# LayerNorm statistics computed per token in five columns and spread back by products, with early buffers for one weight chunk

## The chip, the cores and the metric

The kernel runs on one core of one Trainium2 chip. The metric is the device time of one execution in microseconds (us), as the median of several runs; lower is better.

## What is computed

One inference step of a two-layer decoder for 512 prompt tokens and 8 sample tokens that share every weight. Each layer has three sub-layers (a SwiGLU feed-forward, a token mixer, a second feed-forward), so there are six, numbered n = 0 to 5: n = 0, 2, 3, 5 are feed-forwards, n = 1 is the attention and retention mixer ("EVEN"), n = 4 the short convolution mixer ("ODD"). Around each of them:

```
h = x * (1 + scale) + shift                       # adaLN modulation
x = layernorm(ALPHA * x + gate * sublayer(h)) * g + b
def layernorm(x): mu = mean(x); var = mean((x - mu)^2); (x - mu) * rsqrt(var + eps)
swiglu(h) = (silu(h @ w_a) * (h @ w_b)) @ w_out
```

D is 1024, the feed-forward width 2816. All is float32.

## The kernel before

**Layout.** x lies in SBUF with features on the partitions: 8 tiles of 128 features (KT = 8), each tile 520 tokens wide, split in two halves of 260 so that a half fits a PSUM bank. All products have tokens as the moving operand, 260 columns at a time.

**Products.** To keep float32 accuracy each operand is split in two float32r parts: hi (rounded, by ScalarE) and lo (the rest, by VectorE for activations and GpSimd for weights), and three products hi*hi, hi*lo, lo*hi are added in PSUM (`product`, L707). Weights come in chunks of 128 output columns: SyncE loads a chunk into raw[k], ScalarE cuts w_hi[k] (L1219 to L1224), GpSimd cuts w_lo[k] (L665 to L669), TensorE uses it; there are two buffers, k = 0 and 1, in turn. Each sub-layer has a first product (into the sub-layer) and a second one (back to D), whose output tiles are added to x by VectorE (`residual`, L1545). In the second product of a feed-forward an output tile takes two chunks, in that of a mixer one. In n = 0, 2 and 3 TensorE also works on pieces of the adaLN matrix between the chunks (L731, L740), and turns the last of their sums right after the norm's products (`turn_group`, L720).

**The norm's statistics.** While the second product runs, VectorE adds the tiles up in tile_sum (L1568). After half of the tiles an approximate mean, `shift`, is made from a product with a 128 x 128 matrix of 1/D (mean_w), which adds over the partitions and spreads the result to all of them. With it VectorE makes x - shift (`distance`, L1570 to L1583), ScalarE squares it (L1186), VectorE adds the squares up in sq_sum. After the last tile, `norm_sums` (L815) makes mean and mean square of all 520 tokens, on all 128 partitions, in two pairs of PSUM banks. `norm_act` (L1188) copies the mean to SBUF. `norm` (L1606) on VectorE subtracts and squares (mean - shift), takes it from the mean square, centres tile 0, and takes the reciprocal of the root that ScalarE made (L1193): each of these works on 128 x 520 elements. GpSimd meanwhile centres tiles 1 to 7 (`centre`, L431; tile 7 after the samples of tile 0).

**Into the next sub-layer.** Per tile: VectorE multiplies x by rdev (`normalise_tile`, L1536), ScalarE makes h for the prompt tokens (L1213), GpSimd makes it for the 8 samples with two small instructions (L451, L454), ScalarE rounds it to h_hi (L1217), VectorE makes h_lo (`low`, L1541). TensorE's `first_products` (L744) takes the tiles as they come and works on the first two chunks at once, the second one four tiles behind (LAG = 4).

**Order of the work.** Every engine runs its own list of instructions in the order in which the program gives them, held only by semaphores. GpSimd's list at a boundary: cut the next product's chunk 0, cut its chunk 1 (`body(0)`, L694), centre, samples. ScalarE's: cuts of the two next chunks at the last two chunks' turns, the squares, norm_act, h and h_hi per tile. SyncE's list for EVEN (`even_loads`, L479): chunks 0 to 3, then the page table, then, after the waits at L503 and L504, eight pages of the key cache, then chunks 4 and 5. The pages lie in SBUF over the region R_ADA.

## Time and profile before

| | us |
|---|---|
| median of 3 runs | 2562.47 |
| lowest, highest | 2559.23, 2563.54 |
| the profiled execution | 2561.66 |
| its span, first to last instruction | 2559.8 |

The profile gives for each engine its busy time, the granted clock of TensorE (1.00 is full speed, 0.50 half), and for each instruction its start and duration. A chain view follows the last instruction back through what released each step. A timeline view lists instructions in order of time and merges equal neighbours: "x4" is four of them, and the duration is that from the first one's start to the last one's end. A float32 product appears as two matmul instructions. Durations of neighbours on one engine may overlap by a few hundredths of a microsecond.

### The profile page before, as it was taken

What the parts mean: (1) busy time and instruction counts of PE and PEld (TensorE: products, weight loads), DVE (VectorE), ACT (ScalarE), POOL (GpSimd) and SP (SyncE); (2) the same over time, 40 slices, a digit from 0 to 9 for tenths busy, and PEclk for the clock granted to TensorE, in tenths of its full rate; (3) what the DMA queues carried; (4) which work ended last, traced back from release to release, by engine and by line L of the source; (5) the groups of instructions that cost most, each with busy time, mean ns of one, the idle gap of its engine ahead of it and who ended that gap; (6) DMA issues with size and microseconds to landing.
All of it is one profiled execution on the core that took longest, in us unless ns stands there. A gap on an engine that the chain in (4) does not pass through costs nothing.

```text
span 2559.8 us, 44523 instructions
## 1 busy us (share of the span) xinstructions
PE 2381.1 (93%) x18440; PEld 2153.4 (84%) x18440; DVE 839.5 (33%) x1020; ACT 731.1 (29%) x1055; POOL 929.7 (36%) x473
## 2 busy tenths in 40 slices
PE   7999999989988988899999799999979987999996
PEld 2899988769964338899999799998869986999995
DVE  1122211337434655322212522220253445222214
ACT  3222211242222332422212432221233224222213
POOL 1344433334330014444433444443243435444442
PEclk9999999979986989999999999999989998999998
DMA  7133376526642532233364133347622321333331
GB/s 280 58 91 93 93 238 211 155 72 205 180 118 55 155 94 75 66 91 90 93 213 147 41 95 93 92 141 235 211 72 75 96 78 50 91 93 93 99 91 45
DMA packets 448317, 298.41 MB, mean 117 GB/s; under 512 B 20102, under 2 KB 422118, under 8 KB 448086
## 3 DMA queue, kind: packets, MB, share of 16 engines
q1 hardware_dynamic: 448214, 296.92, 38.0%
q8 instruction: 78, 1.28, 0.2%
q14 instruction: 25, 0.20, 0.0%
HBM read 291.36 MB, written 5.53 MB: 116 GB/s over the span
## 4 chain that ended last, share of the span: by engine, by line
PE 57%; DVE 6%; issue 4%; POOL 3%; ACT 1%; DMA 0%; POOLq 0%; DVEq 0%; SPq 0%; ACTq 0%
PE ps L715 49%; PE ps L740 1%; POOL w_lo L668 1%; POOL x L438 1%; PE ps L1022 1%; DVE sq L1577 1%; PE ps L976 1%; PE ps L972 1%; DVE sq_sum L1582 1%; POOL samp_t L451 1%; DVE x L1539 1%; PE ps L1029 0%; PE ps L727 0%; PE ps L997 0%; DVE rdev L1618 0%
## 5 line engine op out<-in xcount | busy, mean ns | idle before, releaser
L668 POOL TENSOR_TENSOR w_lo<-raw,w_hi 128x1024 fp32r<-128x1024 f32 (+1 forms) x308 | 807.7, 2624 | 1355.5 <-ACT w_hi L1224 1355.5
L715 PE MATMUL ps<-h_hi,w_hi 128*128 128x260 f32 x3584 | 727.3, 284 | 25.0 <-POOL w_lo L668 14.1
L715 PE MATMUL ps<-h_hi,w_lo 128*128 128x260 f32 x3584 | 725.7, 284 | 0.0
L715 PE MATMUL ps<-h_lo,w_hi 128*128 128x260 f32 x3584 | 724.9, 284 | 0.0
L1224 ACT ACTIVATE w_hi<-raw 128x1024 fp32r<-128x1024 f32 (+1 forms) x308 | 346.6, 1126 | 1209.2 <-PE ps L715 1128.4
L715 PEld LDWEIGHTS ps<-h_hi,w_hi 128*128 128x128 f32 x3584 | 556.5, 190 | 30.2 <-POOL w_lo L668 13.4
L715 PEld LDWEIGHTS ps<-h_hi,w_lo 128*128 128x128 f32 x3584 | 556.2, 190 | 0.0
L715 PEld LDWEIGHTS ps<-h_lo,w_hi 128*128 128x128 f32 x3584 | 555.2, 190 | 0.0
L715 PE MATMUL ps<-hid_hi,w_hi 128*128 128x260 f32 x1408 | 296.3, 292 | 0.0
L715 PE MATMUL ps<-hid_hi,w_lo 128*128 128x260 f32 x1408 | 284.1, 283 | 0.0
L715 PE MATMUL ps<-hid_lo,w_hi 128*128 128x260 f32 x1408 | 283.3, 283 | 0.0
L1905 DVE TENSOR_TENSOR gated<-silu_a,ps 128x520 f32<-128x520 f32 x88 | 61.3, 697 | 662.1 <-PE ps L715 646.7
L715 PEld LDWEIGHTS ps<-hid_hi,w_hi 128*128 128x128 f32 x1408 | 216.3, 189 | 47.4 <-issue 42.4
L1908 DVE TENSOR_TENSOR hid_lo<-gated,hid_hi 128x520 f32 (+1 forms) x88 | 204.3, 2322 | 81.9 <-ACT hid_hi L1466 81.9
L715 PEld LDWEIGHTS ps<-hid_lo,w_hi 128*128 128x128 f32 x1408 | 217.5, 189 | 0.0
L715 PEld LDWEIGHTS ps<-hid_hi,w_lo 128*128 128x128 f32 x1408 | 217.4, 189 | 0.0
L1552 DVE SCALAR_TENSOR_TENSOR x<-ps,mod,x 128x512 f32<-128x512 f32 x48 | 36.0, 751 | 538.5 <-PE ps L715 538.5
L756 PE MATMUL ps<-h_hi,w_hi 128*128 128x260 f32 x192 | 48.4, 338 | 61.2 <-DVE h_lo L1543 61.0
L756 PEld LDWEIGHTS ps<-h_hi,w_hi 128*128 128x128 f32 x192 | 33.9, 218 | 74.2 <-issue 58.9
L1577 DVE TENSOR_TENSOR sq<-x,shift 128x520 f32<-128x520 f32 x48 | 81.4, 1706 | 1.4
L740 PE MATMUL ps<-ada_w,c_act 128*32 128x256 f32 x960 | 76.1, 391 | 2.7 <-DMA ada_w<-w_ada 2.7
L684 POOL TENSOR_TENSOR proj<-proj 128x520 f32<-128x520 f32 x4 | 5.1, 1288 | 187.3 <-ACT hn_sq L1340 187.3
(284 smaller groups left out, 1888.0 us busy)
## 6 DMA issues: line engine op xcount, KB each, us to landing
raw<-w_ffn_in SPq DMA_DIRECT2D x176, 512.0 KB, 3.6
ada_w<-w_ada SPq DMA_DIRECT2D x120, 512.0 KB, 6.5
raw<-w_ffn_out SPq DMA_DIRECT2D x64, 704.0 KB, 4.5
pages<-cache_k SPq DMA_DIRECT2D x64, 256.0 KB, 2.9
pages<-cache_v SPq DMA_DIRECT2D x64, 256.0 KB, 2.9
raw<-w_in_even SPq DMA_DIRECT2D x28, 512.0 KB, 4.3
raw<-w_in_odd SPq DMA_DIRECT2D x24, 512.0 KB, 3.6
ada_first<-w_ada SPq DMA_DIRECT2D x5, 2048.0 KB, 14.4
```

What stands on the lines that cost most here:

```text
L438: eng.tensor_tensor(x[:, t], x[:, t], mean[:, :, :], ALU.subtract).then_inc(centred[part], 1)
L451: pool.tensor_tensor(two(samp_t[:, t]), x[:, t, :, HP:HT], two(mod[:, m, KT + t, 1:9]), ALU.mult).then_inc(samp_mod, 1)
L668: pool.tensor_tensor(w_lo[:, k, 0:kt, :], raw[:, k, 0:kt, :], w_hi[:, k, 0:kt, :].bitcast(F32), ALU.subtract).then_inc(chunk_cut, 1)
L715: mm = pe.matmul(ps[:, 2 * q + half, 0:HT], w[:, k, t, :], v[:, kt0 + t, half, :], start=start and t == 0 and step == 0, stop=stop and t = ...
L740: mm = pe.matmul(ps[32 * t:32 * t + 32, 7, 0:ADA_W], c_act[:, at, :], ada_w[:, q % NADA, t, :], start=at < KT // 2, stop=at >= KT // 2)
L756: mm = pe.matmul(ps[:, 2 * q + half, 0:HT], w[:, k, t, :], v[:, t, half, :], start=t == 0 and step == 0, stop=t == KT - 1 and step == 2)
L972: pe.matmul(ps[:, u % 2, 0:(j + 1) * 128], proj[r, QF + m, j * 128:(j + 1) * 128], proj[r, KF + m, 0:(j + 1) * 128], start=True, stop=True ...
L1224: act.activation(w_hi[:, k, 0:kt, :], raw[:, k, 0:kt, :], ACT.Identity).then_inc(hi_cut, 1)
L1552: dve.scalar_tensor_tensor(xt[:, :, 0:HP], ps[:, 2 * q:2 * q + 2, 0:HP], g[:, 0:1], xt[:, :, 0:HP], ALU.mult, ALU.add).then_inc(drained, 1)
L1577: dve.tensor_tensor(sq[:, t % 2], x[:, t], shift[:, :, :], ALU.subtract).then_inc(shifted, 1)
L1905: dve.tensor_tensor(gated[:, j], silu_a[:, j], pair(2 * j + 1), ALU.mult).then_inc(gate_done, 1)
L1908: dve.tensor_tensor(hid_lo[:, m].rearrange("p a h c -> p (a h) c"), gated[:, j], hid_hi[:, m].rearrange("p a h c -> p (a h) c").bitcast(F3 ...
```

## The change

The norm's sums are now made with tokens on the partitions: the data (128 features x 128 tokens) is the stationary operand and one column of mean_w the moving one, so that each product gives one column, and five of them cover the 520 tokens. The fifth block overlaps the fourth. The sum of the tiles is replaced by tile_dev = tile_sum - 8 * shift, made by VectorE before the last residual, whose sums with those of x tile 7 give mean - shift. Square, difference, root and reciprocal run on 128 x 5 elements. The reciprocal is spread back to all partitions, tokens along the free axis, by six products of its columns (broadcast) with parts of the identity, into a PSUM pair that `normalise_tile` then reads. The mean itself is still made by products with mean_w and copied to SBUF for the centring; its part of tile_sum no longer waits for the last tile. The add of square 6 moves ahead of the last residual. In n = 0 and 3 the last turn_group moves ahead of the spread. Chunk 1 of each next first product is loaded into early_raw and cut into early_hi and early_lo, in the region R_ADA, while the second product still runs: SyncE issues it before the last two chunks, ScalarE cuts it at the third chunk from the end, GpSimd right after the last chunk of the second product. ScalarE runs a root on a small tile at the last-but-one chunk. In EVEN, SyncE waits for both first chunks to be used before it loads pages.

```diff
+        early_raw = put("early_raw", [128, KT, 128], F32, R_ADA)
+        early_hi = put("early_hi", [128, KT, 128], F32R, R_ADA + 4096)
+        early_lo = put("early_lo", [128, KT, 128], F32R, R_ADA + 8192)
+        tile_dev = put("tile_dev", [128, 2, HT], F32, R_ADA + 3 * 4096 + 1024)
...
+        tok = new("tok", [128, 4, TB])
+        delta_sq, dev, root, rdev = (tok[:, u] for u in range(4))
...
+        def token_block(v, b):
+            at = min(128 * b, NTOK - 128)
+            return v.rearrange("p h c -> p (h c)")[:, at:at + 128]
...
+            def early_chunk(n):
+                if n + 1 < last:
+                    sp.dma_start(early_raw[:, :, :], early_view(n + 1)).then_inc(early_full, 16)
...
                 sp.wait_ge(ada_turned, groups_before(EVEN))
+                sp.wait_ge(chunk_used, c0 + 2)
                 for k in range(2):
                     granule(cache_k, 0, k)
...
+            def early_cut(n):
+                if n + 1 < last:
+                    pool.wait_ge(early_hi_cut, n + 1)
+                    pool.tensor_tensor(early_lo[:, :, :], early_raw[:, :, :], early_hi[:, :, :].bitcast(F32), ALU.subtract)
...
+                        second_body(KT // 2 - 1)
+                        early_cut(n)
                     else:
-                        body(0)
                         if n:
-                            centre(pool, n - 1, 1)
+                            cut(chunks_before(n), 0, KT, 2)
+                            centre(pool, n - 1)
...
             def norm_sums(n):
+                def per_token(bank, v, start):
+                    for b in range(TB):
+                        mm = pe.matmul(ps[:, bank, b:b + 1], token_block(v, b), mean_w[:, 0:1], start=start and b == 0,
+                                       stop=not start and b == TB - 1)
+                    return mm
                 pe.wait_ge(shift_ready, n + 1)
-                pe.wait_ge(samp_added, KT * (n + 1))
+                pe.wait_ge(summed, (KT - 1) * (n + 1))
                 for half in range(2):
                     pe.matmul(ps[:, 4 + half, 0:HT], mean_w, tile_sum[:, half, :], start=True, stop=False)
+                pe.wait_ge(delta_steps, 3 * n + 1)
+                per_token(0, tile_dev[:, :, :], True)
+                pe.wait_ge(samp_added, KT * (n + 1))
+                per_token(0, x[:, KT - 1], False).then_inc(mean_done, 1)
+                for half in range(2):
                     mm = pe.matmul(ps[:, 4 + half, 0:HT], mean_w, x[:, KT - 1, half, :], start=False, stop=True)
                 mm.then_inc(mean_done, 1)
                 pe.wait_ge(sq_added, (KT - 2) * (n + 1))
+                per_token(1, sq_sum[:, :, :], True)
+                pe.wait_ge(squared, KT * (n + 1))
+                per_token(1, sq[:, (KT - 1) % 2], False).then_inc(var_done, 1)
+                if ADAS[n]:
+                    turn_group(n, GROUPS * len(ADAS[n]) - 1)
+                pe.wait_ge(mean_ready, n + 1)
+                pe.wait_ge(centred[0], CENTRE * (n + 1))
+                pe.wait_ge(rdev_done, n + 1)
                 for half in range(2):
-                    pe.matmul(ps[:, half, 0:HT], mean_w, sq_sum[:, half, :], start=True, stop=False)
-                pe.wait_ge(squared, KT * (n + 1))
-                for half in range(2):
-                    mm = pe.matmul(ps[:, half, 0:HT], mean_w, sq[:, (KT - 1) % 2, half, :], start=False, stop=True)
+                    bank = 2 * spread_pair(n) + half
+                    for b, at, cols, out0 in (((0, 0, 128, 0), (1, 0, 128, 128), (2, 0, 4, 256)),
+                                              ((2, 4, 124, 0), (3, 0, 128, 124), (4, 120, 8, 252)))[half]:
+                        mm = pe.matmul(ps[:, bank, out0:out0 + cols], rdev[:, b:b + 1].to_broadcast([128, 128]),
+                                       ident[:, at:at + cols], start=True, stop=True)
...
-                        if not beyond or next_kt:
-                            cut(c0 + s + 2, u % 2, next_kt if beyond else kt)
+                        if not beyond:
+                            cut(n, c0 + s + 2, u % 2, kt)
+                        elif u % 2 == 0:
+                            act.activation(root, eps_ln[:, :].to_broadcast([128, TB]), ACT.Sqrt)
+                            if next_kt:
+                                cut(n, c0 + s + 2, 0, next_kt, 2)
+                        if s + 3 == KT * per_tile:
+                            early_cut(n)
...
-                dve.tensor_tensor(x[:, t], x[:, t], rdev[:, :, :], ALU.mult).then_inc(normed, 1)
+                dve.tensor_tensor(x[:, t], x[:, t], pair(spread_pair(n)), ALU.mult).then_inc(normed, 1)
...
+                    if t == KT - 1:
+                        dve.wait_ge(summed, (KT - 1) * (n + 1))
+                        dve.scalar_tensor_tensor(tile_dev[:, :, :], shift[:, :, :], -float(KT), tile_sum[:, :, :], ALU.mult, ALU.add
+                                                 ).then_inc(delta_steps, 1)
                     product_done(t // 2, t % 2)
...
                 dve.wait_ge(mean_ready, n + 1)
-                dve.tensor_tensor(shift[:, :, :], mean[:, :, :], shift[:, :, :], ALU.subtract).then_inc(delta_steps, 1)
-                dve.wait_ge(delta_steps, d0 + 1)
-                dve.tensor_tensor(shift[:, :, :], shift[:, :, :], shift[:, :, :], ALU.mult).then_inc(delta_steps, 1)
+                for t in range(CENTRE):
+                    dve.tensor_tensor(x[:, t], x[:, t], mean[:, :, :], ALU.subtract).then_inc(centred[0], 1)
+                dve.wait_ge(var_done, 2 * n + 1)
                 dve.wait_ge(delta_steps, d0 + 2)
-                dve.wait_ge(var_done, n + 1)
-                dve.tensor_tensor(dev, pair(0), shift[:, :, :], ALU.subtract).then_inc(delta_steps, 1)
-                centre(dve, n, 0)
+                dve.tensor_tensor(dev, ps[:, 1, 0:TB], delta_sq, ALU.subtract).then_inc(delta_steps, 1)
                 dve.wait_ge(dev_done, n + 1)
-                dve.reciprocal(rdev[:, :, :], dev).then_inc(rdev_done, 1)
-                dve.wait_ge(rdev_done, n + 1)
+                dve.reciprocal(rdev, root).then_inc(rdev_done, 1)
+                dve.wait_ge(var_done, 2 * n + 2)
```

## Rows read from the trace of the kernel before

**Rows 1.** The page: the chain that ended last, by engine.
```profile
PE 57%; DVE 6%; issue 4%; POOL 3%; ACT 1%; DMA 0%; POOLq 0%; DVEq 0%; SPq 0%; ACTq 0%
```

**Rows 2.** Timelines (start, us, engine), norm of n = 2: VectorE, ScalarE, GpSimd, ScalarE.
```profile
1439.34 0.17 DVE L1557 TENSOR_TENSOR x<-x,samp 128x8 f32<-128x8 f32 x1
...
1441.68 0.60 ACT L1190 ACTIVATE mean<-ps 128x520 f32<-128x520 f32 x1 [0.77 <-PE ps L822]
...
1442.41 9.32 POOL L438 TENSOR_TENSOR x<-x,mean 128x520 f32<-128x520 f32 x6
...
1455.80 0.64 ACT L1217 ACTIVATE h_hi<-h 128x520 fp32r<-128x520 f32 x1 [1.13 <-POOL h L454]
```

**Rows 3.** Narrow float32 products: TensorE's timeline, then the chain in order of time.
```profile
1432.42 0.51 PE L727 MATMUL ps<-res,ada_sums 128*128 128x9 f32 x4
...
748.12 4.41 PE ps L905 x20
```

**Rows 4.** TensorE's timeline, wide float32 products in the norm of n = 1.
```profile
1014.14 1.07 PE L822 MATMUL ps<-x,res 128*128 128x260 f32 x2
1015.01 1.07 PE L821 MATMUL ps<-tile_sum,res 128*128 128x260 f32 x2
```

**Rows 5.** Timelines of GpSimd and VectorE, single instructions, norm of n = 1.
```profile
1020.79 1.74 POOL L438 TENSOR_TENSOR x<-x,mean 128x520 f32<-128x520 f32 x1
1022.49 1.28 POOL L438 TENSOR_TENSOR x<-x,mean 128x520 f32<-128x520 f32 x1
...
1019.72 0.70 DVE L1615 TENSOR_TENSOR sq<-ps,shift 128x520 f32<-128x520 f32 x1
```

**Rows 6.** Timelines of GpSimd and ScalarE, tile 3 after the norm of n = 2.
```profile
1457.86 0.74 POOL L451 TENSOR_TENSOR samp_t<-x,mod 128x8 f32<-128x8 f32 x1 [1.65 <-DVE x L1539]
1458.68 0.54 POOL L454 TENSOR_TENSOR h<-samp_t,mod 128x8 f32<-128x8 f32 x1
...
1459.31 0.64 ACT L1217 ACTIVATE h_hi<-h 128x520 fp32r<-128x520 f32 x1 [0.68 <-POOL h L454]
```

**Rows 7.** TensorE's timeline, norm of n = 0; then ScalarE, h_hi of tile 1.
```profile
505.67 0.71 PE L821 MATMUL ps<-tile_sum,res 128*128 128x260 f32 x2
...
521.75 0.64 ACT L1217 ACTIVATE h_hi<-h 128x520 fp32r<-128x520 f32 x1 [1.13 <-POOL h L454]
```

**Rows 8.** VectorE's timeline, end of the second product of n = 1; then ScalarE, h_hi of tile 1.
```profile
1005.87 2.90 DVE L1577 TENSOR_TENSOR sq<-x,shift 128x520 f32<-128x520 f32 x1
...
1012.83 0.17 DVE L1557 TENSOR_TENSOR x<-x,samp 128x8 f32<-128x8 f32 x1
...
1030.16 0.64 ACT L1217 ACTIVATE h_hi<-h 128x520 fp32r<-128x520 f32 x1 [1.13 <-POOL h L454]
```

**Rows 9.** Timelines of SyncE, TensorE, ScalarE, TensorE, start of EVEN.
```profile
535.78 8.05 SPq L494 DMA_DIRECT2D pages<-cache_k  x8
...
538.57 0.48 PE L715 MATMUL ps<-h_hi,w_hi 128*128 128x260 f32 x2 [0.15 <-POOL w_lo L668]
...
549.25 1.06 ACT L1224 ACTIVATE w_hi<-raw 128x1024 fp32r<-128x1024 f32 x1 [3.34 <-DMA raw<-w_in_even]
...
552.19 0.17 ACT L1239 ACTIVATE proj<-ps 128x8 f32<-128x8 f32 x1
...
553.92 0.60 PE L852 MATMUL ps<-res,proj 128*8 128x128 f32 x4
```

**Rows 10.** Timelines of GpSimd, VectorE and ScalarE, the last norm (n = 5).
```profile
2527.74 11.06 POOL L438 TENSOR_TENSOR x<-x,mean 128x520 f32<-128x520 f32 x7 [14.88 <-ACT mean L1190]
...
2535.15 7.27 DVE L1539 TENSOR_TENSOR x<-x,rdev 128x520 f32<-128x520 f32 x8
...
2539.40 4.37 ACT L1203 ACTIVATE x<-x,params 128x520 f32<-128x520 f32 x6 [0.88 <-DVE x L1539]
```

**Rows 11.** Windows: stretch, us, busy PE, PEld, DVE, ACT, POOL (instructions), PEclk, DMA share, GB/s.
```profile
785.00:792.00 7.00, 7.00 (x129) 6.91 (x128) 2.75 (x7) 0.00 (x0) 0.00 (x0) 0.50 0.28 65
...
1018.60:1029.50 10.90, 0.00 (x0) 0.00 (x0) 9.73 (x8) 2.89 (x4) 10.77 (x10) 0.70 0.05 13
```

114 lines of the change are left out of this document (73 added, 41 removed).

## The prediction

> **What bounds the kernel now.** I read the page first: the chain that ended last runs through TensorE for 57% and through VectorE for 6% [rows 1], and most of that TensorE share is the dense products, which the change leaves as they are. So the question is what TensorE waits for between two sub-layers, six times. I then read the chain in order of time at each norm. In the mixers it leads through GpSimd's centring of six tiles, and ScalarE's rounding (h_hi) of tile 1 waits for GpSimd's sample instruction [rows 8]. The timelines of the engines show why: x tile 0 is centred by VectorE, but GpSimd makes the samples of tile 0 only after its six centrings, and every h_hi waits for its samples. In n = 2 the last sample add ends at T0 = 1439.51, the mean is copied at 1441.68, the six centrings run from 1442.41 to 1451.73, and the h_hi of tile 1 starts at 1455.80 [rows 2]. VectorE's own chain of 520-wide instructions ends at about the same time as the centrings, so both must get shorter for anything to be won. From there the tiles come at a pace that TensorE follows, and the time at which h_hi of tile 1 starts, plus the pace, sets the end. I price each norm by that start.
>
> **Prices.** A narrow float32 product (two records): 20 records of L905 take 4.41 at the low clock, 0.22 each; four records of L727 take 0.51 with the drain, which fits about 0.11 each at the full clock [rows 3]. So a block of five one-column products (10 records) costs 1.1 us at full clock and 2.2 at half. The width of the moving operand hardly enters; I take this from products of 8 and 9 columns, the nearest rows. A page of the Trainium skill speaks otherwise: "TensorE: Matmul & The Clock Gate", in the section "Part 1: The HAM clock gate", gives start-to-start times that fall with the width of the moving operand down to about 25 ns; by that a block would cost an estimated 0.25 us, and the sum would come out several us lower. The rows here, with a new stationary operand each time, do not bear it out, and I keep 0.11 and 0.22. Two 260-column records take 0.87 at the low clock (1014.14 to 1015.01), so four take 1.75, and 0.87 at full clock [rows 4]. A centring on GpSimd takes 1.74 when VectorE works beside it on two SBUF operands, and 1.28 beside the reciprocal, while VectorE's own instruction with one PSUM operand takes 0.70 in the midst of the centrings [rows 5]. So neither blocks the other there. After the change VectorE has only one SBUF-only wide instruction beside the centrings (tile 0): six of them take 1.8 + 5 x 1.24 (1.28 less the overlap) = 8.0 instead of 9.3.
>
> **n = 2.** TensorE ends its last product at about 1438.4 (T0 less the 1.1 us of the residual). Then: tile_sum, 0.9, to 1439.3; block of tile_dev, 1.1, to 1440.4; block of x tile 7, to 1441.5 (T0 is past); its four wide records, to 1442.3; copy of the mean, 0.7, to 1443.05, where before it ended at 1442.3. The first mean thus comes 0.8 later. Centrings to 1451.1. Samples of tile 0, 0.5; tile 7, 1.24; samples of tile 1 (the first behind h_lo of tile 0, 0.66, the second 0.28): h_hi of tile 1 at 1453.75 against 1455.80 [rows 2], a gain of 2.05. The statistics are hidden: 20 records for the squares to 1444.5, three small instructions, about 0.9 with their handovers, spread of 12 records 1.3 to 2.6, done by 1448.1 at the worst, 3 us before the centrings end. If that cover went, each further us would cost one.
>
> **The pace.** Two tiles take 3.51 (h_hi from 1455.80 to 1459.31). In that pair, tile 3 waits for two sample instructions of 0.74 and 0.54, the second held up by normalise_tile [rows 6]. With a PSUM operand the latter no longer holds the port, so 0.54 becomes 0.20: 0.34 less per pair, in two pairs; the last has no normalise_tile behind it. Gain 0.7 per norm. For n = 2 together -2.75.
>
> **n = 0 and 3.** Here TensorE still works on the adaLN pieces until 505.67 [rows 7]. From there 0.9, 1.1, 1.1, 0.9 and 0.7 give the mean at 510.35; centrings to 518.3; with 0.5, 1.24 and 0.94, h_hi of tile 1 at 521.0 against 521.75 [rows 7]. Gain 0.8 + 0.7 = 1.5 each, -3.0 for both. The moved turn_group (0.4) lies under the centrings.
>
> **n = 1 and 4, the mixers.** Their second product has one chunk per tile, and VectorE is behind TensorE: an SBUF-only subtract takes 2.90 because a weight cut of GpSimd has the port [rows 8]. The early cut comes just before and takes the port once more, 2.3 us of VectorE time, while the cut it replaces lay after T0. Add 6 before the last residual waits for its square (0.15) and takes 0.62, tile_dev 0.75. Behind VectorE's list stand the last residual and, for it, TensorE. T0 moves from 1013.0 [rows 8] by 3.8 to 1016.8. TensorE has by then been idle long enough that the clock is at its half level: in a stretch without any product its mean is 0.70, full at first and half for the rest [rows 11]. So: tile_dev to 1017.9, x tile 7 to 1020.05, wide records to 1021.8, mean 1022.5, centrings to 1030.5. The spread comes at 1021.8 + 4.3 + 0.9 + 2.6 = 1029.6, normalised tile 0 at 1030.3, again just covered. h_hi of tile 1: 1030.5 + 0.5 + 1.24 + 0.94 = 1033.2 against 1030.16 [rows 8], 3.0 later, less 0.7 of pace: +2.3 each, +4.6.
>
> **EVEN's pages.** The new wait moves the page loads from 535.78 to the end of the first two products, about 538.4 (TensorE starts the third at 538.57). Chunk 4 is queued behind them on SyncE; ScalarE cuts it at 549.25 having waited for its DMA, and only then copies chunks 2 and 3, to 552.36, which TensorE's L852 needs at 553.92 [rows 9]. 2.65 later is 1.1 late: +1.1. Were it hidden, 0; were more behind it, 2.65. The other queues: early chunks are as large as those they replace, are issued chunks ahead of their cuts, and cost nothing; the new root and its table load on ScalarE come a whole chunk before anyone waits for it.
>
> **The last norm.** By the steps of n = 2 the mean comes 0.7 later: seven centrings from 2528.4, in 9.25, to 2537.7 instead of to 2538.8. Before, normalising starts only at 2535.15 and takes 7.27 for eight tiles, and ScalarE's last affine ends at 2543.77 [rows 10]. Now the spread is there by 2532.2 to 2533.4, every tile follows its centring, the last affine ends at 2537.7 + 0.65 + 0.85 = 2539.2: -4.5.
>
> **Clock allowance.** The one-column products may not hold the clock up: in the stretch of 128 one-column products TensorE is busy 7.00 of 7.00 us and stays at 0.50 [rows 11]. If it falls in the middle of the blocks before the mean, 1 to 3 us per feed-forward norm; after the last dense product the full level outlasts part of an idle stretch [rows 11], and the blocks come first in it, so I add 1.0 in all.
>
> **Sum.** -2.75 - 3.0 + 4.6 + 1.1 - 4.5 + 1.0 = -3.5 against the profiled execution's 2561.66 (span 2559.8 and 1.9 around it). The median of the runs shown is 0.8 above that, so 2562.5 - 3.5 = 2559.0. About 0.2%, 5.1 us, is what a measurement of this kernel can tell from no change; this lies within it.
>
> **Rivals.**
> 1. *The early cut costs the mixers nothing like 3.8.* For it: the port is free between two cuts for longer than a cut takes, so one more cut may fall in a gap. Against: the 2.90 subtract shows the queue is tight [rows 8]. If T0 moves by 1.5 only, 4.6 less: 2554.4, faster. Chance 0.25.
> 2. *The clock falls as soon as the dense products end.* Place: the blocks before the mean in n = 0, 2, 3, 5. Price: 1.1 + 1.1 + 0.9 = 3.1 each, 12.4 less the allowance: 2559.0 + 11.4 = 2570, slower. It turns the sign at 1.1 us per norm and passes 0.2% at 2.4. For it: rows 11, first row. Against: the second of them, in which the full level outlasts the products. Chance 0.12. The page named above says in the same section that the throttled state is the default and activity releases it; the first of rows 11 agrees only if one-column products are not much activity, and read as plain busy time it would speed the mixers up by some 2 us each, an estimate from the two prices above.
> 3. *It does not do what it says: GpSimd's list stays the bound.* If the centrings keep 1.74, because VectorE's instructions hold GpSimd up whatever their operands, six take 10.2 instead of 8.0, 2.2 more in five norms, and seven 2.7 more in the last: 2559.0 + 11.0 + 2.7 = 2572.7, slower. Against: 1.28 beside the reciprocal [rows 5]. Chance 0.05.
> 4. *A one-column product costs far less than 0.22 and 0.11*, the page's way. As a mechanism here: if the load of the stationary operand hides behind the product before, a block costs 0.3 instead of 1.1 or 2.2, twice before each mean: 1.6 less in four norms, 3.7 in two: 2545. The two values of rows 3 speak against it, the width being hardly in them. Chance 0.03.
>
> My forecast has 0.55.
>
> **How the numbers follow.** The predicted time is the forecast's, 2559.0. Its own range, 2555 to 2565, takes in the page wait (0 to 2.65), the clock (0 to 4) and T0 of the mixers (2.5 to 5 each). To leave out no more than 2 in 10 it reaches to rival 1 below and to two thirds of rival 2's price above: 2552.5 to 2567. Faster by over 0.2% (below 2557.3): rivals 1 and 4 and a tenth of the forecast, 0.33. Slower (above 2567.6): rivals 2, 3 in most of their width, 0.15. Within: 0.52.
>
> **What would show it.** Right: h_hi of tile 1 some 14.3 us after T0 in n = 2 (before 16.3), with GpSimd idle before its first sample for less than 0.1; five of six centrings at 1.28; T0 to last product end in the mixers grown by nearly 4 and the mean 5 later; sample instructions at 0.20 where 0.54 stood; the last affine within 2 of the last centring; L852 waiting for ScalarE. Wrong: PEclk below 1.00 before the mean in the feed-forward norms; records of the blocks at other than 0.11 and 0.22; the spread ending after the centrings; L1577 in the mixers no longer than before in sum.

## The result, and the profile after

The changed kernel takes 2568.43 us (median of 7 executions, 2566.33 to 2572.74) against 2562.47 for the kernel before on the same chip: a ratio of 1.0028, 95% interval 1.0016 to 1.0040, slower by 6.0 us. I had forecast 2559.0, in a range from 2552.5 to 2567: 3.5 us faster, where it is 6.0 slower. The profiled execution of the changed kernel is its slowest (2572.74, span 2570.6), so the two profiles are 10.8 us apart where the medians are 6.0 apart.

The table cuts both traces at the same places: "product" is everything from the first dense product behind one norm's first two chunks to the end of the last dense product before the next norm; "norm" is the rest. Times in us, from TensorE's timeline.

| stretch | before | after | difference | forecast |
|---|---|---|---|---|
| start to last product of n = 0 | 504.4 | 508.2 | +3.8 | 0 |
| norm of n = 0 | 34.2 | 32.6 | -1.6 | -1.5 |
| EVEN (products of n = 1) | 470.7 | 475.2 | +4.6 | +1.1 |
| norm of n = 1 | 37.3 | 39.9 | +2.6 | +2.3 |
| products of n = 2 | 391.9 | 392.6 | +0.7 | 0 |
| norm of n = 2 | 33.7 | 31.0 | -2.7 | -2.75 |
| products of n = 3 | 418.2 | 420.9 | +2.6 | 0 |
| norm of n = 3 | 34.1 | 32.6 | -1.5 | -1.5 |
| ODD (products of n = 4) | 191.7 | 192.6 | +0.9 | 0 |
| norm of n = 4 | 37.6 | 39.9 | +2.3 | +2.3 |
| products of n = 5 | 370.0 | 370.0 | 0 | 0 |
| last norm to the end | 36.0 | 35.0 | -1.0 | -4.5 |

Five norms came out as forecast. What I missed lies ahead of the norms of n = 0 and 3, in EVEN, and in the last norm. A single profile has to be read with care in two rows. The stretch up to the last product of n = 0 takes from 504.4 to 507.9 us in the eleven profiles of this document that have no late early cut, a spread that stands before 390 us into the kernel. EVEN takes from 467.7 to 473.0 in the nine without the page wait. In the two profiles compared here the first stretch runs alike, within 0.2 us, up to 482 us, and in each of the three profiles with the late cut 3.7 to 3.8 us are lost between 385 us and the last product.

The changed kernel's timelines in the norm of n = 2, against [rows 2]: TensorE, ScalarE, GpSimd, ScalarE, and GpSimd again for tile 3 [rows 6].

```profile
1449.29 1.17 PE L875 MATMUL ps<-res,tile_dev 128*128 128x1 f32 x10
1450.32 1.25 PE L875 MATMUL ps<-res,x 128*128 128x1 f32 x10
...
1452.60 0.60 ACT L1265 ACTIVATE mean<-ps 128x520 f32<-128x520 f32 x1 [0.81 <-PE ps L888]
...
1453.28 8.00 POOL L460 TENSOR_TENSOR x<-x,mean 128x520 f32<-128x520 f32 x6 [8.65 <-ACT mean L1265]
...
1463.94 0.64 ACT L1291 ACTIVATE h_hi<-h 128x520 fp32r<-128x520 f32 x1 [0.79 <-POOL h L476]
...
1466.00 0.75 POOL L473 TENSOR_TENSOR samp_t<-x,mod 128x8 f32<-128x8 f32 x1 [1.32 <-DVE x L1625]
1466.83 0.20 POOL L476 TENSOR_TENSOR h<-samp_t,mod 128x8 f32<-128x8 f32 x1
```

Here the steps hold with their sizes: a block of ten records starts 1.03 us after the one before, the mean comes 0.8 later after T0 than before, six centrings take 8.00 instead of 9.32, and the h_hi of tile 1 starts 14.3 us after T0 (1449.64) where it was 16.3. The second sample instruction of tile 3 takes 0.20 where it took 0.54.

Now the first surprise. Before the last chunk of n = 0 TensorE turns a group of adaLN sums (L727, now L777), and for it waits for ScalarE's copy of them. The timelines of the kernel before: TensorE, ScalarE, VectorE.

```profile
490.28 0.61 PE L727 MATMUL ps<-res,ada_sums 128*128 128x9 f32 x4 [1.48 <-ACT ada_sums L1393]
...
489.32 0.64 ACT L1186 ACTIVATE sq<-sq 128x520 f32<-128x520 f32 x1 [0.70 <-DVE sq L1577]
489.86 0.37 ACT L1393 ACTIVATE ada_sums<-ps 128x256 f32<-128x256 f32 x1
...
486.52 0.69 DVE L1582 TENSOR_TENSOR sq_sum<-sq_sum,sq 128x520 f32<-128x520 f32 x1
```

The same place in the changed kernel: TensorE, ScalarE, GpSimd, VectorE.

```profile
492.61 0.61 PE L777 MATMUL ps<-res,ada_sums 128*128 128x9 f32 x4 [3.69 <-ACT ada_sums L1473]
...
490.30 0.64 ACT L1259 ACTIVATE sq<-sq 128x520 f32<-128x520 f32 x1 [2.91 <-DVE sq L1663]
491.64 0.64 ACT L1259 ACTIVATE sq<-sq 128x520 f32<-128x520 f32 x1 [0.71 <-DVE sq L1663]
492.19 0.36 ACT L1473 ACTIVATE ada_sums<-ps 128x256 f32<-128x256 f32 x1
...
482.78 3.37 POOL L707 TENSOR_TENSOR w_lo<-raw,w_hi 128x1408 fp32r<-128x1408 f32 x1 [7.37 <-ACT w_hi L1298]
486.10 2.86 POOL L714 TENSOR_TENSOR early_lo<-early_raw,early_hi 128x1024 fp32r<-128x1024 f32 x1
...
483.00 3.71 DVE L1663 TENSOR_TENSOR sq<-x,shift 128x520 f32<-128x520 f32 x1
486.64 2.89 DVE L1674 TENSOR_TENSOR sq_sum<-sq_sum,sq 128x520 f32<-128x520 f32 x1
```

Read it from the bottom. GpSimd runs its early cut right behind another cut. VectorE's addition of squares, 0.69 in the kernel before with no GpSimd instruction beside it, takes 2.89 meanwhile. So its next two subtractions come 2.3 later, ScalarE's squares of them too, and the copy of the sums stands behind these squares in ScalarE's queue: 492.19 instead of 489.86. TensorE waits 3.69 instead of 1.48. Section 8, "Key points", of the page "GPSIMD Engine Reference" in the Trainium skill says that GpSimd shares its SBUF interfaces with VectorE and that they contend when a VectorE instruction has two SBUF inputs; this trace agrees, 2.89 against 0.69.

The wait costs more than its length. Windows of the changed kernel (stretch, us, then busy PE, PEld, DVE, ACT, POOL, PEclk, DMA):

```profile
490.00:492.00 2.00, 0.00 (x0) 0.00 (x0) 1.97 (x4) 0.99 (x2) 0.00 (x0) 1.00 0.00 0
492.00:494.00 2.00, 1.40 (x14) 0.96 (x15) 1.53 (x3) 1.97 (x4) 0.00 (x0) 0.98 0.00 0
494.00:496.00 2.00, 2.00 (x11) 2.00 (x11) 0.00 (x0) 0.07 (x1) 0.00 (x0) 0.50 0.00 0
496.00:498.00 2.00, 2.00 (x17) 1.61 (x16) 0.00 (x0) 0.25 (x1) 0.00 (x0) 0.67 0.00 0
```

Behind 3.7 us without a product the granted clock falls to 0.50 (1.2 GHz) in the midst of dense products, for 3.4 us, and is back at 1.00 before 498; in the kernel before it stayed at 1.00 here. That is some 1.6 us more by difference: 2.2 + 1.6 = 3.8.

At n = 3 the changed kernel has the same wait of 3.69 for the same copy, but there the clock fell in the kernel before too, behind its wait of 1.48. The windows behind the wait, kernel before, then changed kernel:

```profile
1876.00:1880.00 4.00, 4.00 (x26) 3.65 (x26) 0.00 (x0) 0.17 (x1) 0.00 (x0) 0.57 0.00 0
...
1883.00:1890.00 7.00, 6.40 (x34) 5.30 (x38) 1.53 (x3) 2.12 (x5) 0.00 (x0) 0.51 0.00 0
```

The clock stays at 0.50 for 3.4 us before and for 6.8 now. Of the eleven profiles with the wait of 1.48 at n = 3, eight have such a fall of 3.4 us and three have none; at n = 0 none of the eleven has one, and all three with the wait of 3.7 do. So the clock fell at the end of all six long waits or just behind it, and behind eight of 22 short ones.

The mixers went as forecast, with the last residual (T0) 7.3 us behind the last product instead of 3.8. The end of the norm of n = 1, TensorE and ScalarE, against [rows 8]:

```profile
1022.49 2.29 PE L875 MATMUL ps<-res,tile_dev 128*128 128x1 f32 x10 [5.58 <-DVE tile_dev L1691]
1024.64 2.27 PE L875 MATMUL ps<-res,x 128*128 128x1 f32 x10
...
1040.23 0.64 ACT L1291 ACTIVATE h_hi<-h 128x520 fp32r<-128x520 f32 x1 [0.70 <-POOL h L476]
```

The last norm, against [rows 10]: TensorE, GpSimd, VectorE, ScalarE.

```profile
2537.36 1.25 PE L875 MATMUL ps<-res,x 128*128 128x1 f32 x10
2538.47 2.07 PE L888 MATMUL ps<-x,res 128*128 128x260 f32 x4
2540.34 2.13 PE L875 MATMUL ps<-res,sq_sum 128*128 128x1 f32 x10
2542.33 2.27 PE L875 MATMUL ps<-res,sq 128*128 128x1 f32 x10
2545.50 2.70 PE L903 MATMUL ps<-res,tok 128*128 128x128 f32 x12 [0.90 <-DVE tok L1711]
...
2541.26 9.24 POOL L460 TENSOR_TENSOR x<-x,mean 128x520 f32<-128x520 f32 x7 [16.61 <-ACT mean L1265]
...
2548.24 4.93 DVE L1625 TENSOR_TENSOR x<-x,ps 128x520 f32<-128x520 f32 x8 [2.88 <-PE ps L903]
...
2548.97 5.80 ACT L1277 ACTIVATE x<-x,params 128x520 f32<-128x520 f32 x8 [3.84 <-DVE x L1625]
```

TensorE is busy from the last product to 2544.6, and from 2538.5 on at half the clock: blocks of 1.2 take 2.2. Normalising starts 11.6 us after T0 (2536.67); I had the spread done at 7.3 to 8.5, and before, normalising started at 10.3. The centrings are no longer what it waits for. In EVEN, against [rows 9], SyncE, ScalarE and TensorE:

```profile
541.72 8.13 SPq L520 DMA_DIRECT2D pages<-cache_k  x8
...
555.22 1.06 ACT L1298 ACTIVATE w_hi<-raw 128x1024 fp32r<-128x1024 f32 x1 [7.10 <-DMA raw<-w_in_even]
...
558.38 1.01 PE L927 MATMUL ps<-res,proj 128*8 128x128 f32 x4 [2.03 <-ACT proj L1319]
```

The pages start 0.9 us after the third product (540.79), where they had started 2.8 ahead of it: 3.7 later, not 2.65, and L927 (L852 before) waits 2.03 for ScalarE, where it had not waited.

### The profile page after: what moved, and what is told of

It reads as the page before. It is cut to its first block and busy times, and to the rows that moved or that the text cites. A ratio compares the mean times of both kernels' runs of the same rounds, so it can differ in the third digit from the quotient of the medians.

```text
span 2570.6 us, 44965 instructions
## 1 busy us (share of the span) xinstructions
PE 2429.2 (94%) x18704; PEld 2204.1 (86%) x18704; DVE 800.7 (31%) x1014; ACT 727.2 (28%) x1067; POOL 912.9 (36%) x473
## 5 line engine op out<-in xcount | busy, mean ns | idle before, releaser
L707 POOL TENSOR_TENSOR w_lo<-raw,w_hi 128x1024 fp32r<-128x1024 f32 (+1 forms) x303 | 792.3, 2616 | 1327.8 <-ACT w_hi L1298 1327.8
L765 PE MATMUL ps<-h_hi,w_hi 128*128 128x260 f32 x3584 | 727.7, 284 | 25.7 <-POOL w_lo L707 16.4
L1298 ACT ACTIVATE w_hi<-raw 128x1024 fp32r<-128x1024 f32 (+1 forms) x303 | 341.3, 1127 | 1208.4 <-PE ps L765 1115.7
L765 PEld LDWEIGHTS ps<-h_hi,w_hi 128*128 128x128 f32 x3584 | 557.4, 190 | 30.2 <-POOL w_lo L707 13.5
L460 POOL TENSOR_TENSOR x<-x,mean 128x520 f32<-128x520 f32 x42 | 55.6, 1354 | 76.4 <-ACT mean L1265 76.4
L1473 ACT ACTIVATE ada_sums<-ps 128x256 f32<-128x256 f32 x60 | 22.6, 376 | 163.4 <-PE ps L790 163.2
```

Source lines behind the costliest of these rows:

```text
L460: pool.tensor_tensor(x[:, t], x[:, t], mean[:, :, :], ALU.subtract).then_inc(centred[1], 1)
L707: pool.tensor_tensor(w_lo[:, k, 0:kt, :], raw[:, k, 0:kt, :], w_hi[:, k, 0:kt, :].bitcast(F32), ALU.subtract).then_inc(chunk_cut, chunks)
L765: mm = pe.matmul(ps[:, 2 * q + half, 0:HT], w[:, k, t, :], v[:, kt0 + t, half, :], start=start and t == 0 and step == 0, stop=stop and t = ...
L1298: act.activation(w_hi[:, k, 0:kt, :], raw[:, k, 0:kt, :], ACT.Identity).then_inc(hi_cut, chunks)
L1473: act.activation(ada_sums[:, :], ps[:, 7, 0:ADA_W], ACT.Identity).then_inc(rows_copied, 1)
```

## The experiments

Times are medians beside the kernel before on the same chip, with the ratio and its 95% interval. A difference of two experiments is that of the means of their executions, its interval by resampling them. Experiments 1 to 4 ran on one chip, 5 to 7 on a second, 8 and 9 on a third, 10 on a fourth. Taking each against its own kernel before moves these differences by 0.1 us at most, except for fill against t0_free (-0.5 or -1.9) and mean_ahead against mean_wide_fill (+1.5 or +2.5), and widens their intervals.

**1. stats_only.** The statistics without the early buffers: both first chunks by way of the shared buffers, no wait ahead of the pages.

```
-                    sp.dma_start(early_raw[:, :, :], early_view(n + 1)).then_inc(early_full, 16)
...
-                sp.wait_ge(chunk_used, c0 + 2)
...
-                            cut(chunks_before(n), 0, KT, 2)
+                            body(0)
```

> The changed kernel without its buffers for the second chunk: both first chunks go through the shared buffers again, GpSimd cuts both of them before it centres, and the wait ahead of the pages is gone; the token-column statistics stay. Theory A (the early cut is what costs: it delays VectorE's and ScalarE's squares at n=0 and 3, the last residual of the mixers, and the first pages of EVEN; the statistics by themselves pay): by segments of the two traces the early cut cost +3.8 and +2.6 us before the last product of n=0 and 3, about 3.6 us at each mixer norm and +4.6 in EVEN; the statistics alone should give about -2 us at n=2, -1.5 at n=0 and 3, -1.2 at each mixer, -0.5 at the last norm: some -8 us, 2554.5 us. The last product of n=0 ends near 504.4 us. Rival B (the clock that falls under one-column products is the loss, the early cut is harmless): 2566 us or more.

Measured 2554.31 us, ratio 0.9972 (0.9961 to 0.9982): faster than both kernels, and what theory A said. Its sum was right with parts that were not: the two mixer norms got 0.5 and 0.2 us longer and not 1.2 shorter, and the last one 2.8 shorter and not 0.5, which happens to cancel. TensorE's wait before the last chunk of n = 0 is back at its old length:

```profile
493.79 0.61 PE L788 MATMUL ps<-res,ada_sums 128*128 128x9 f32 x4 [1.48 <-ACT ada_sums L1484]
```

The products of n = 3 take 417.4 (changed kernel 420.9), the last norm to the end 33.3, that of n = 2 31.0. One sentence of the expectation was a miss: the last product of n = 0 ends at 507.9, not 504.4. This profile is behind from early on, in a stretch that no edit touches (its first dense product starts at 89.0 us, where it was 86.9, and at 385 us it is the full 3.5 behind); the wait itself is what to compare. Another surprise is in the mixers: T0 is still 6.45 us behind the last product.

**2. early_only.** The kernel before with the early buffers, cuts and page wait.

> The kernel before with the early buffers, the early cut and the wait ahead of the pages, its statistics as they were. Theory A: the early cut costs +3.8, +2.6, 2 x 3.6 and +4.6 us and gives back under 1 us a norm (no second cut between last product and first product): 2572 to 2577 us, the last product of n=0 near 508 us. Rival B: 2558 to 2563 us, nothing lost before the last product of n=0.

Measured 2574.86 us, ratio 1.0053 (1.0040 to 1.0065): 13 us slower than before. The stall is there with the old statistics, at n = 0 and alike at n = 3:

```profile
496.47 0.61 PE L766 MATMUL ps<-res,ada_sums 128*128 128x9 f32 x4 [3.70 <-ACT ada_sums L1443]
```

The two halves add up: -7.5 and +13.0 make +5.5, and the whole change measured +6.0. In the mixers T0 is 5.9 us behind the last product, so the early cut alone makes it 2.2 later.

**3. early_moved.** The changed kernel with the early load and cuts in the middle of the second product.

```
-                        if s == 2 * KT - 2:
+                        if s == 4:
                             early_chunk(n)
...
+                            with pool.Fori(0, 2) as i:
+                                second_body(i)
+                            early_cut(n)
+                            with pool.Fori(2, KT // 2) as i:
+                                second_body(i)
...
-                        if s + 3 == KT * per_tile:
+                        if s == (5 if n in FFN else 1):
                             early_cut(n)
```

> The changed kernel with the early load, ScalarE's early cut and GpSimd's early cut taken from the end of the second product to its middle (feed-forward: with chunk 5 of 16; mixers: with chunk 1 of 8), before VectorE begins its squares; the wait ahead of the pages stays. Theory A: the stall before the last chunk of n=0 and 3 goes (-3.8 and -2.6 us) and the mixers' last residual comes 3.6 us earlier each, EVEN's +4.6 stays: 2568.4 - 13.6 = 2554.8 us. Rival C (the delay at these places is the new order of VectorE's additions, one more between two squares, and not the early cut): 2568 us.

Measured 2558.14 us, ratio 0.9986 (0.9977 to 0.9995), 10.3 less than the changed kernel by nothing but the place of the early load and its two cuts. The wait at n = 0 is 1.47. The products of n = 3 take 417.2, and sort all profiles: 420.4 to 421.5 in the three kernels with the early cut at the end, 416.7 to 418.2 in the eleven others. Of the 13.6 us expected 3 did not come: T0 in the mixers fell from 7.3 to 5.2 us behind the last product, and not to 3.8, and the mixer norms from 39.9 to 37.7.

**4. mean_first.** The changed kernel with TensorE's wide product of the last tile, and so the mean, ahead of the two blocks of the deviation. ScalarE's copy of the mean and its square of the deviation change places too, and in the last norm GpSimd's last centring waits for that square.

```
+                pe.wait_ge(samp_added, KT * (n + 1))
+                for half in range(2):
+                    mm = pe.matmul(ps[:, 4 + half, 0:HT], mean_w, x[:, KT - 1, half, :], start=False, stop=True)
+                mm.then_inc(mean_done, 1)
                 pe.wait_ge(delta_steps, 3 * n + 1)
                 per_token(0, tile_dev[:, :, :], True)
-                pe.wait_ge(samp_added, KT * (n + 1))
                 per_token(0, x[:, KT - 1], False).then_inc(mean_done, 1)
-                for half in range(2):
-                    mm = pe.matmul(ps[:, 4 + half, 0:HT], mean_w, x[:, KT - 1, half, :], start=False, stop=True)
-                mm.then_inc(mean_done, 1)
```

> The changed kernel with TensorE's order turned: the wide product with the last tile, and so the mean that starts all centring, comes before the two one-column blocks of the deviation, not behind them. Theory D (centring starts from the mean and sets the first normalised tile in five of six norms): the mean comes 0.8 to 2 us earlier where it was 3 to 4.5 us behind the last residual, so -0.8 at n=2, -2 at n=0 and 3, -2 at each mixer, 0 at the last norm: about -6 to -8 us, 2561 us. Rival E (the chain of one-column products on a clock of 0.50, then the square root and the spread, sets the start): no gain, 2567 to 2570 us.

Measured 2571.84 us, ratio 1.0035 (1.0023 to 1.0047): rival E, and not even better than the changed kernel (+1.5 us, -1.0 to +3.8). The mean did come earlier, 2.2 us after T0 in the mixers where it was 5.5. But from the mean to the first normalised tile it is now 11.9 there and 7.9 to 9.3 elsewhere, where it was 6.6 to 7.7: behind the mean stand 40 one-column records at up to 0.22 each, and they set the start. The profile is less even than the time: the norms of n = 0, 2, 3 and 5 are 0.8, 1.5, 1.1 and 0.9 us shorter than in the changed kernel, those of the two mixers 0.8 longer, 2.8 less in sum, which the times of eight executions don't bear out. Centring and statistics are two chains of nearly one length; shortening one gives the difference and no more.

**5. wide_tokens.** stats_only with each one-column product made TW = 32 columns wide, 31 of them of no use.

```
-                        mm = pe.matmul(ps[:, bank, b:b + 1], token_block(v, b), mean_w[:, 0:1], start=start and b == 0,
+                        mm = pe.matmul(ps[:, bank, TW * b:TW * b + TW], token_block(v, b), mean_w[:, 0:TW], start=start and b == 0,
```

> The kernel of run stats_only with every one-column product made 32 columns wide (32 equal columns, of which one is read). Theory F (a one-column product costs its stationary operand, so that more columns ride along, and the clock falls because so few columns move): a product stays at 0.11 us warm and the granted clock stays at 1.00 through the blocks of the feed-forward norms, where the last block now takes 2.27 us; -1 to -3 us, 2552 us. Rival G (the columns cost their passes): a block of ten goes from 1.2 to 1.7 us or more, the mean is 0.8 to 1.5 us later in each of six norms: 2559 to 2562 us.

Measured 2553.05 us, ratio 0.9964 (0.9951 to 0.9978); against stats_only -1.4 us (-3.6 to +0.8). The profile is clearer than the time. TensorE's timeline in the last norm:

```profile
2522.32 1.28 PE L887 MATMUL ps<-res,x 128*128 128x32 f32 x10
2523.44 1.12 PE L900 MATMUL ps<-x,res 128*128 128x260 f32 x4
2524.40 1.20 PE L887 MATMUL ps<-res,sq_sum 128*128 128x32 f32 x10
2525.43 1.28 PE L887 MATMUL ps<-res,sq 128*128 128x32 f32 x10
```

And windows of the same stretch, in which the number behind the five busy times is the granted clock (PEclk):

```profile
2523.00:2524.00 1.00, 1.00 (x9) 0.94 (x9) 0.00 (x0) 0.22 (x2) 0.00 (x0) 1.00 0.00 0
2524.00:2526.00 2.00, 2.00 (x19) 1.94 (x17) 0.70 (x1) 0.60 (x1) 0.72 (x1) 1.00 0.00 0
```

Thirty-two columns take as long as one (a block of ten 1.20 to 1.28, against 1.17 to 1.25), and the clock stays at 1.00 to the end of the blocks, where the changed kernel had 0.50. So the width of such a product is free here, and in all four feed-forward norms of this profile the blocks end before the clock falls, where in stats_only, with TensorE just as busy, it fell during them in all four. That is not assured by the width: in mean_wide (experiment 9), 32 wide as well, it fell at n = 0 before the last block, with TensorE busy throughout.

```profile
512.01 2.32 PE L889 MATMUL ps<-res,sq 128*128 128x32 f32 x10
```

Of the 16 feed-forward norms in the four kernels with 32 columns, 11 end their blocks before the clock falls; of the 32 in the eight with one column, 2. The last norm to the end takes 31.9 us instead of 33.3: 4.2 less than before, near the -4.5 I had forecast. In the norms of n = 0, 2 and 3 the first normalised tile starts 1.6 to 3.0 earlier, and their lengths do not change by 0.1: GpSimd's centrings and samples set those.

**6. t0_free.** stats_only with the last addition of squares and the deviation of the sums behind the last residual of the mixers.

```
-                if t == KT - 2:
+                if t == KT - 2 and n in FFN:
                     add_squares(n, t)
+                if t == KT - 1 and n not in FFN:
+                    add_squares(n, t - 1)
...
-                    if t == KT - 1:
+                    if t == KT - 1 and n in FFN:
+                        deviation()
...
                     residual(n, t // 2, t % 2, t % 2)
+                    if t == KT - 1 and n not in FFN:
+                        deviation()
```

> The kernel of run stats_only (token-column statistics, no early buffers) with two VectorE operations of each mixer moved behind the last residual, where the kernel before had the one of them that it had: the last addition of squares and the deviation of the sums. Theory H (these two, in front of the last residual and slowed or kept waiting by GpSimd's two cuts, are what makes the last residual late): in stats_only the last residual ends 6.46 and 6.45 us behind the last product of the mixers, 3.76 before; it comes back to 3.8, -2.7 us each, of which the two operations behind it give back up to 1.4 where TensorE waits for the deviation: -3 to -5.4 us, 2549 to 2551.5 us. Rival I (the chain behind the last residual waits for TensorE's products or GpSimd anyway, so the earlier residual is eaten): within 1 us of stats_only, 2554 us.

Measured 2553.28 us, ratio 0.9965 (0.9951 to 0.9979); against stats_only -1.6 us (-3.9 to +0.5), so the times alone leave it open. The trace does not: T0 is 3.76 and 3.74 us behind the last product, as theory H said, and the mean then 7.07 behind T0 instead of 4.33, so that the mixer norms take 37.87 and 37.84 where they took 37.81. The two operations cause the late residual, and moving them gives nothing: TensorE's block of tile_dev ran ahead of the residual in stats_only (from 2.2 us before T0), and now starts 0.7 us behind it, because it reads the deviation that was moved, and takes 2.3 on a clock at 0.50. Rival I. What an earlier residual would give with the deviation left ahead of it, this run cannot say.

**7. page_wait and no_even_early.** stats_only with the page wait alone; and early_moved without an early chunk for EVEN, and so without the wait.

```
+                sp.wait_ge(chunk_used, c0 + 2)
                 for k in range(2):
                     granule(cache_k, 0, k)
```

> The kernel of run stats_only with the change's wait ahead of the pages alone (SyncE waits for the use of EVEN's second chunk, about 6 us, before it loads the first pages and the chunks behind them). Theory J (the +4.6 us in EVEN of the changed kernel's profile is this wait): 2558 to 2559 us. Rival K (the transfers have slack there, and that profile was a slow one of its kind): 2554 to 2555.5 us, my +1.1 or less.

> The kernel of run early_moved without an early chunk for EVEN, and so without the wait ahead of the pages; the early chunks of the other four products stay, loaded and cut in the middle of the second product. Theory J: the 3.8 us between early_moved (2558.1) and stats_only (2554.3) are the pages: 2554 us. Rival L (they are what four early chunks cost by themselves in the middle of the products): 2557.5 us.

Measured 2557.22 (0.9987, 0.9977 to 0.9998) and 2553.60 us (0.9968, 0.9958 to 0.9978). The wait adds 3.5 us to stats_only (1.5 to 5.4), and taking it out of early_moved gives 3.9 (2.3 to 5.3). Theory J by size: 3 to 4 us, not my 1.1. The length of EVEN in a single profile does not show it: its products take 471.2 with the wait and 471.3 without, and between 467.7 and 473.0 in nine profiles that have no wait, so +4.6 in the table above is partly that execution. The start of EVEN does show it. The product of L852 (L927 in the changed kernel) starts 15.35 us after the third product in all nine and does not wait; in the five profiles with the page wait it starts 16.9 to 18.3 after it, having waited 1.4 to 2.8 us. The first product on proj and even_t, some 200 us into EVEN, starts at 197.1 to 199.0 in the nine and at 199.6 to 202.9 in the five. And no_even_early stands within 0.6 us of stats_only (-2.4 to +1.4): moved out of the way, four early chunks cost nothing and bring nothing.

**8. fill.** t0_free with five wide products of no use in the mixers' idle stretch.

```
                     pe.matmul(ps[:, 4 + half, 0:HT], mean_w, tile_sum[:, half, :], start=True, stop=False)
+                if n not in FFN:
+                    for u in range(5):
+                        pe.matmul(ps[:, 0, 0:HT], mean_w, tile_sum[:, u % 2, :], start=True, stop=True)
```

> The kernel of run t0_free with five wide products of no use (sums of the tiles into a bank that the token columns overwrite) between the last product and the last residual of each mixer, 2.6 us in which TensorE stood idle. Theory M (at the mixers TensorE comes to the statistics from an idle stretch with a clock of 0.50, and its blocks take 2.1 to 2.3 us for ten columns where 1.2 is to be had): the last residual to mean falls from 7.07 to 4.5 us or so and the norm of a mixer from 37.85 to 34.5 to 36 us: -4 to -6 us, 2548 us. Rival N (the clock falls in the blocks whatever went before them): within 1 us of t0_free, 2553 us, or above it where the fillers run late.

Measured 2550.73 us, ratio 0.9959 (0.9944 to 0.9975), by times not distinct from t0_free. TensorE's timeline in the norm of n = 1:

```profile
1010.13 2.35 PE L896 MATMUL ps<-tile_sum,res 128*128 128x260 f32 x10
1013.82 1.28 PE L886 MATMUL ps<-res,tile_dev 128*128 128x1 f32 x10 [1.33 <-DVE tile_dev L1709]
1014.96 1.25 PE L886 MATMUL ps<-res,x 128*128 128x1 f32 x10
1016.08 1.95 PE L902 MATMUL ps<-x,res 128*128 128x260 f32 x4
```

The first two blocks take 1.3, no longer 2.3, and the mixer norms 35.7 and 36.2 us instead of 37.8: theory M, at the small end of its size or just past it, because the clock fell again 3.1 and 2.5 us after T0: in the first of them behind 20 one-column records, so that the four wide records take 1.95.

**9. mean_wide and mean_wide_fill.** t0_free with the edits of experiments 4 and 5, without and with the fillers of 8.

> The kernel of run t0_free with the mean's product first (mean_first) and the token columns 32 wide (wide_tokens); no fillers. Theory O (the first normalised tile waits for whichever is later, GpSimd's seven centrings from the mean or the one-column chain; with the clock kept at 1.00 the chain takes 8.0 to 8.5 us from the mean and no longer sets it): in the feed-forward norms the mean moves 1.6 to 2.2 us forward and the norms with it, n=0 and 3 from 32.56 to 30.3, n=2 from 31.0 to 29.5, the last one from 33.3 to 31; the mixers, on a cold clock, stay at 37 to 38 us: -8 us, 2545 us. Rival E (the chain still sets it): -3 us or less, 2550 us.

> mean_wide with the five fillers at the mixers. Theories M and O together: each mixer norm 3.8 + 1.4 + 27 = 32.2 us where it takes 37.8, some -11 us more: 2534 us. Rival N: as mean_wide, 2545 us.

Measured 2548.68 (0.9936, 0.9918 to 0.9955) and 2544.11 us (0.9924, 0.9910 to 0.9938); the fillers are worth 3.9 (0.6 to 6.9). mean_wide_fill is the best version found, 0.76% under the kernel before, but 10 us above its expectation. VectorE, ScalarE and TensorE in its norm of n = 1 show what holds the mixers at 34.7 us instead of 32.2:

```profile
1011.98 2.85 DVE L1682 TENSOR_TENSOR sq<-x,shift 128x520 f32<-128x520 f32 x1
...
1014.86 0.64 ACT L1276 ACTIVATE sq<-sq 128x520 f32<-128x520 f32 x1 [3.34 <-DVE sq L1682]
1015.41 0.59 ACT L1280 ACTIVATE mean<-ps 128x520 f32<-128x520 f32 x1
...
1011.51 1.14 PE L902 MATMUL ps<-x,res 128*128 128x260 f32 x4 [0.72 <-DVE x L1662]
```

The mean is in PSUM by 1012.7 and is copied at 1015.4, behind a square that waits for a subtraction beside GpSimd's cut. The rest is the last norm at 32.7 and those of n = 2 and 3 at 30.2 and 31.3, where I had 31, 29.5 and 30.3.

**10. mean_ahead.** mean_wide_fill with that copy ahead of the square. The copy also waits for the deviation here.

```
                 act.activation(mean[:, :, :], pair(2), ACT.Identity).then_inc(mean_ready, 1)
+                if n not in FFN:
+                    squares(n, (KT - 1,))
...
-                            squares(n, SQUARES_WITH[t])
+                            if t < KT - 1 or n in FFN:
+                                squares(n, SQUARES_WITH[t])
```

> mean_wide_fill with one turn more at the mixers: ScalarE copies the mean before it squares the last tile, which VectorE hands it only 3.4 us behind the last residual (its subtraction runs beside GpSimd's cut and takes 2.85 us). Theory P (the mean stood ready in PSUM and its copy was queued behind that square): last residual to mean falls from 3.95 to 1.5 us; GpSimd ends its cut 2.8 us behind the last residual, so centring starts some 1.3 us earlier and each mixer norm takes 33.4 us instead of 34.7: -2.6 us, 2541.5 us. Rival Q (the statistics, whose last square is now behind the copy, take over): each mixer norm at 34.2 to 35 us, 2544 us.

Measured 2546.22 us, ratio 0.9930 (0.9917 to 0.9944): rival Q. Against mean_wide_fill that is no gain (+1.5 us, -1.0 to +3.9). Last residual to mean fell from 3.95 to 1.24, but from there to the first normalised tile it is 10.7 and 11.5 us instead of 6.1 and 6.8:

```profile
1018.17 1.77 DVE L1700 TENSOR_TENSOR sq_sum<-sq_sum,sq 128x520 f32<-128x520 f32 x1
1019.86 1.78 DVE L1736 TENSOR_TENSOR x<-x,mean 128x520 f32<-128x520 f32 x1
...
1017.65 8.85 POOL L468 TENSOR_TENSOR x<-x,mean 128x520 f32<-128x520 f32 x6
```

Centring now starts while VectorE still has two-operand instructions to do: 1.77 and 1.78 where 0.69 and 0.70 stood, and 8.85 for the centrings instead of 7.98. The add of squares, at 1.77, ends later, so TensorE starts its block of them 5.1 us after T0 instead of 4.0; the last square is later too, and the first normalised tile comes 1.8 and 2.0 later after T0 than in mean_wide_fill. Mixer norms 35.0 and 35.7.

## Why the prediction was wrong

It said -3.5, within noise; the result is +6.0. The two profiles are 14.3 us further apart than forecast (10.8 against -3.5): 6.4 of it ahead of the norms of n = 0 and 3, 3.5 in EVEN, 3.5 in the last norm, the rest in small amounts. By its steps:

- **"The other queues: early chunks ... cost nothing".** This failed, and is the largest part of the error: the sum has no term for the products of n = 0 and 3, that is, it puts them at nothing, and gives no reason. The reason given, the size and the time of the loads, speaks for SyncE's queue alone and not for GpSimd's cut of the same chunk. I priced the early cut's hold on VectorE in the mixers and did not ask who waits for VectorE in the feed-forward products. T0 is not late there, but another instruction stood in the line: the copy of the adaLN sums, behind ScalarE's squares, that TensorE waits for in n = 0 and 3. The row for it (1.48 <-ACT ada_sums) was in the trace of before, a wait that the 2.3 us of VectorE's delay lengthened by 2.2. Price: 2.2 us of wait and 1.6 of clock at n = 0; 3.4 at n = 3 (420.9 against stats_only's 417.4), of which 2.2 are wait. With the cut moved, the wait is 1.47 again (early_moved); with the cut alone, it is 3.70 (early_only).
- **EVEN's pages, +1.1.** The wait was put in the right place and mis-sized: 3.5 us (1.5 to 5.4) by page_wait. I moved the loads by 2.65 and let ScalarE have 1.5 of slack; they moved by 3.7 in the changed kernel's trace, L852 comes 1.5 to 3.0 us late in five profiles, and the runs don't tell which transfer behind them costs the rest. My upper bound of 2.65 lies below both estimates (3.5 and 3.9), though inside the intervals of both.
- **The last norm, -4.5.** It was -1.0 in the profile of the changed kernel, -2.8 in stats_only. "Every tile follows its centring" failed: the one-column chain set the start, and there the clock fell in the blocks. This was the mechanism of rival 2, but at another place: it does not cost the norms of n = 0, 2 and 3 anything (wide_tokens: 31.0 with and without), where GpSimd hides it, and costs the last one 1.4 (stats_only) to 3.2 us (the changed kernel). The clock allowance of 1.0 was too small for that one and not needed for the others.
- **n = 0, 2 and 3, -5.75 together.** Right in size: -1.6, -2.7, -1.5, with 8.0 for six centrings and the 0.34 a pair of tiles (h_hi of tile 1 to tile 3 takes 3.18 at n = 3 where it took 3.51). At n = 0 and 3 part is luck: the h_hi of tile 1 comes only 0.4 to 0.5 us earlier after T0, not 0.8, and some 0.5 that no step forecast is won behind it. Rival 3 is out.
- **The mixers, +4.6.** Right in sum (+2.6 and +2.3) and in T0 (+3.6, forecast 3.8), from parts that were not: I gave the early cut 2.3 and the two VectorE operations 1.5 and added them. Alone, the early cut makes T0 2.2 later (early_only) and the two operations 2.7 (stats_only); together 3.6, so they overlap, and the operations were priced too low. Rival 1, T0 later by 1.5 only, is out.
- **Prices.** 0.11 and 0.22 for a narrow record held, and rival 4 is out: a start-to-start of 0.10 at the full clock and 0.20 to 0.215 at half, at one column and at 32.

The early buffers' purpose would have been to have less between mean and centring. In the kernel before, GpSimd began its centrings 0.7 us after the copy of the mean at every norm, so its second cut was not in the way of the centrings. With the old statistics the early buffers brought the h_hi of tile 1 forward by 0.5 to 0.6 us after T0 in n = 0, 2 and 3 (early_only), with the new ones nothing that the times show (no_even_early against stats_only); there were 14 us to lose, the page wait among them.

Not settled: how much of the page wait's price lies in which transfer, and why the granted clock falls at a different point of the blocks, and at n = 3 behind a wait of 1.48 or not, in different profiles. Every reading of a trace here is of one execution of a kernel.

## What to carry to other kernels

When an engine gets a piece of work "off the path", list what shares its ports or stands behind its victims, at every place that the piece runs, and look for waits that are short but not zero: TensorE's 1.48 was the sign. A change of two halves should be timed as two, since here one was worth -7.5 us and the other +13.0. And where two chains start at one event (centring and statistics), moving the event or shortening one gives only the gap between them.

## What the runs showed of the hardware

- A float32 product record with a new stationary operand each time takes 0.10 us at full clock (2.4 GHz) and 0.20 to 0.215 at half (1.2 GHz), whether 1 or 32 columns move. One wide, in the last norm of the changed kernel, the clock went to 0.50 from about 2538.5 on, 2.9 us behind the last dense product, with TensorE busy all the time. Made 32 wide, the blocks of wide_tokens ran to their end at 1.00 in all four feed-forward norms; over all profiles that holds for 11 of 16 norms at 32 columns and 2 of 32 at one.
- An idle stretch of 3.7 us in dense products was followed by 0.50 for 3.4 us at n = 0 in three of three profiles. One of 1.5 us was not at n = 0 (none of eleven), but was at n = 3 (eight of eleven).
- Section "Part 1: The HAM clock gate" of "TensorE: Matmul & The Clock Gate" in the Trainium skill says that activity releases the throttle. These runs agree for the dense products, under which the clock returned to 1.00 (by 498 at n = 0), and show a TensorE that was busy without a gap and was throttled all the same (changed kernel, 2538.5 to 2544.6).
- Five useless wide products (2.35 us) in an idle stretch kept the clock at 1.00 until 3.1 us after T0 at n = 1, where it had fallen 0.2 us before T0 (t0_free), and the two blocks behind them took 1.3 instead of 2.3.
- A VectorE addition of 520 elements with both inputs in SBUF took 0.69 us alone, 2.89 beside a GpSimd cut of 1024 elements, and 1.77 beside GpSimd's centrings.
